# Moving transfers, waits and pieces of work at the layer ends of a two-layer attention and delta-rule trunk

## The reference

```python
mod = silu(c) @ w_ada + b_ada                 # shift, scale, gate; a second set from c_ctx
p   = (rmsnorm(x) * (1 + sc) + sh) @ w_in     # one projection for both groups of heads
# group A, 8 heads: differential softmax attention with rotary positions, SiLU gate
# group B, 8 heads: short convolution, chunked gated delta rule in both directions, SiLU gate
x   = x + gt * (concat([y_a, y_b]) @ w_out)   # the same for ctx, in the first layer only
```

## Time and profile before

| | |
|---|---|
| median of three runs | 2666.12 us (2658.32 to 2667.49) |
| the profiled execution, its own time | 2668.75 us |
| its span in the profile | 2666.9 us |
| granted TensorE clock, mean | 0.952 |
| busy share of PE, DVE, ACT, POOL | 89%, 53%, 35%, 4% |
| HBM traffic over the span | 123 GB/s |

### The profile page before, as it was taken

One profiled execution on the slowest core, in us unless ns is written; L12 is line 12 of the kernel. 1 busy time (PEld: TensorE's weight loads), 2 busy tenths in 40 slices (PEclk: granted clock), 3 DMA queues, 4 the chain that ended last, 5 costly groups with the idle time before them and its releaser, 6 DMA issues. The chain is left out here.

```text
span 2666.9 us, 40817 instructions
## 1 busy us (share of the span) xinstructions
PE 2373.2 (89%) x14870; PEld 1958.8 (73%) x14870; DVE 1413.2 (53%) x2409; ACT 924.6 (35%) x1727; POOL 102.3 (4%) x155
## 2 busy tenths in 40 slices
PE   6799999999989998999899689889898989889696
PEld 3278787878777877778688468778687877778685
DVE  1334646454555546464653554655666555655555
ACT  3434233242424242332412354242423424242422
POOL 0000000000000000000000000000000000000000
PEclk8999999999999999999899799999999999999897
DMA  8964444443434344443434445243433334233353
GB/s 322 353 174 120 112 121 107 112 123 99 119 91 127 84 116 106 127 107 95 150 112 146 150 107 141 68 115 79 111 99 92 97 88 125 74 102 84 114 154 123
DMA packets 553603, 329.72 MB, mean 124 GB/s; under 512 B 48658, under 2 KB 517814, under 8 KB 552710
## 3 DMA queue, kind: packets, MB, share of 16 engines
q1 hardware_dynamic: 393174, 218.59, 29.9%
q10 hardware_dynamic: 160240, 109.13, 14.1%
q0 software_dynamic: 64, 0.20, 0.0%
HBM read 304.73 MB, written 23.13 MB: 123 GB/s over the span
## 5 line engine op out<-in xcount | busy, mean ns | idle before, releaser
L1678 PE MATMUL ps<-h_hi,w_hi 128*128 128x512 f32 (+1 forms) x2080 | 835.2, 402 | 25.3 <-DVE h_lo L1037 12.6
L1679 PE MATMUL ps<-h_lo,w_hi 128*128 128x512 f32 (+1 forms) x2080 | 772.6, 371 | 0.0
L1680 PE MATMUL ps<-h_hi,w_lo 128*128 128x512 f32 (+1 forms) x2080 | 771.6, 371 | 0.0
L1037 DVE TENSOR_TENSOR w_lo<-w_raw,w_hi 128x1024 fp32r<-128x1024 f32 (+1 forms) x332 | 399.0, 1203 | 391.9 <-ACT w_hi L594 337.0
L594 ACT CAST w_hi<-w_raw 128x1024 fp32r<-128x1024 f32 (+1 forms) x332 | 341.2, 1030 | 544.5 <-PE ps L1680 153.7
L1678 PEld LDWEIGHTS ps<-h_hi,w_hi 128*128 128x128 f32 x2080 | 403.7, 194 | 121.1 <-issue 41.5
L1680 PEld LDWEIGHTS ps<-h_hi,w_lo 128*128 128x128 f32 x2080 | 401.8, 193 | 69.6
L1679 PEld LDWEIGHTS ps<-h_lo,w_hi 128*128 128x128 f32 x2080 | 404.8, 195 | 48.2
L1037 DVE TENSOR_TENSOR arena<-arena,ps 128x512 f32<-128x512 f32 (+1 forms) x192 | 117.7, 641 | 131.9 <-PE ps L1763 130.7
L1931 PE MATMUL ps<-h_hi,w_hi 128*128 128x512 f32 (+1 forms) x448 | 159.1, 355 | 6.8 <-DVE arena L1493 6.8
L1762 PE MATMUL ps<-arena 128*128 128x128 f32 x512 | 111.5, 303 | 50.7 <-DVE arena L1037 26.2
(11 more groups left out here) (189 smaller groups left out, 2738.9 us busy)
## 6 DMA issues: line engine op xcount, KB each, us to landing
w_raw<-in_w_in SPq DMA_DIRECT2D x260, 512.0 KB, 4.2
ada_raw<-in_w_ada ACTq DMA_DIRECT2D x128, 512.0 KB, 5.3
w_raw<-in_w_out SPq DMA_DIRECT2D x64, 448.0 KB, 3.8
arena<-in_w_ada SPq DMA_DIRECT2D x27, 512.0 KB, 8.3
w_raw<-in_w_ada SPq DMA_DIRECT2D x19, 512.0 KB, 8.3
ada_raw<-in_w_ada SPq DMA_DIRECT2D x18, 512.0 KB, 8.3
arena<-decay_rows ACTq DMA_DIRECT2D x16, 512.0 KB, 4.8
x_channel_major<-arena ACTq DMA_DIRECT2D x1, 4096.0 KB, 17.6
```

The lines of the kernel that those rows point to most:

```text
L1037: return V.tensor_tensor(o, a, b, op)
L1678: mm(o, w_hi[:, s, k], h_hi[:, kt, t0:], start=kt == 0, stop=False)
L1679: mm(o, w_hi[:, s, k], h_lo[:, kt, t0:], start=False, stop=False)
L1680: last = mm(o, w_lo[:, s, k], h_hi[:, kt, t0:], start=False, stop=kt == KT - 1)
```

## The change

- Order on SP: the block writes go from before unit 6 to before unit 7, `blocks_back` from before unit 8 or 9 to before unit 10; in the last body from after units 5 and 9 to after 7 and 11 (layer 0) or 8 and 13 (layer 1).
- `ADA_SLOT` of layer 0: 19, 44, 50 and 56 become 18, 46, 51 and 57.
- Last body: the pieces are spread from slot 2 on, not 8, and stand behind the plan of a slot on PE; the first four units are taken as half 0 of tiles 0 and 1, then half 1 of both. Groups 0 and 1 of y are loaded one unit earlier than groups 2 and 3, which need the last unit used; the splits of y move from slots 3, 4, 6, 7 to 0, 1 (2 on DVE), 4, 6.
- x blocks use four buffers in `ada_raw` in place of two in the arena. Blocks 0 to 7 of x are loaded for the tail in slot 38 of the last body (`old_load`).
- POOL sums the squares in place of DVE.
- Layer 1: the split of unit `base + 3` moves ahead of the modulation, and PE multiplies the first tile of body 0 (AV, units `base + 2` and `base + 3`) block by block beside the decay tile; slots 0 to 7 of body 0 project nothing.

Only added and removed lines are shown, with the line number of the kernel before.

```diff
@@ 238 @@
-x_part = (cin.rearrange("p s n -> p (s n)")[:, 0:T], th)
+x_part = [ada_raw[:, s // 2, 4 * (s % 2):4 * (s % 2) + 4].rearrange("p k n -> p (k n)") for s in range(4)]
@@ 426 @@
-ADA_SLOT, ADA_EARLY = {0: (9, 14, 19, 44, 50, 56), 1: (10, 17)}, {0: 3, 1: 2}
-BLOCKS_OUT, BLOCKS_BACK = {0: 6, 1: 6}, {0: 8, 1: 9}
+ADA_SLOT, ADA_EARLY = {0: (9, 14, 18, 46, 51, 57), 1: (10, 17)}, {0: 3, 1: 2}
+BLOCKS_OUT, BLOCKS_BACK = {0: 7, 1: 7}, {0: 10, 1: 10}
...
+def out_unit(u):
+    return (u % 2, u // 2) if u < 4 else (u // 2, u % 2)
+def last_unit(n):
+    return n + 2 if n < 2 else 2 * n + 1
...
-    return 8 + p * (SLOTS - 8) // (2 * OUT_UNITS)
+    return 2 + p * (SLOTS - 2) // (2 * OUT_UNITS)
...
-    return min(piece_slot(4 * n + 3) + 1, SLOTS - 1)
+    return min(piece_slot(2 * last_unit(n) + 1) + 1, SLOTS - 1)
+OUT_BLOCKS = {0: (7, 11), 1: (8, 13)}
@@ 549 @@
-half, n = u % 2, u // 2
+n, half = out_unit(u)
...
-    sp.wait_ge(w_used, first)
-    sp.wait_ge(ya_stored, 16 * (HEADS * layer + OUT_HEADS))
-    sp.wait_ge(yb_stored, 16 * (HEADS * layer + OUT_HEADS))
...
+        if g == 0:
+            sp.wait_ge(w_used, first - 1)
+            sp.wait_ge(ya_stored, 16 * (HEADS * layer + OUT_HEADS))
+        if g == 2:
+            sp.wait_ge(w_used, first)
+            sp.wait_ge(yb_stored, 16 * (HEADS * layer + OUT_HEADS))
...
-if u == 5:
+if u == OUT_BLOCKS[layer][0]:
...
-if u == 9:
+if u == OUT_BLOCKS[layer][1]:
@@ 665 @@
+    split_hi(0, base + LEAD)
...
-    for u in range(1, LEAD):
+    for u in range(1, LEAD + 1):
...
-split_hi(0, base + LEAD)
@@ 907 @@
+    act.wait_ge((ya_ready, yb_ready)[which], h())
...
-        act.wait_ge(qkv_ready, h(-1, 3, 3))
-        act.wait_ge(z_ready, h(-1, 2, 2))
...
-    if n >= 2:
-        act.wait_ge(part_stored[n % 2], 16 * (layer * KT // 2 + n // 2))
-    act.dma_start(x_part[n % 2][:, c0 * P:], x_dram[n, :, c0 * P:]).then_inc(part_loaded[n % 2], 16)
+    if n >= 4:
+        act.wait_ge(part_stored[n % 4], 16 * (layer * KT // 4 + n // 4))
+    act.dma_start(x_part[n % 4][:, c0 * P:], x_dram[n, :, c0 * P:]).then_inc(part_loaded[n % 4], 16)
+def old_load():
+    act.wait_ge(z_ready, h(-1, 2, 2))
+    for b in range(4):
+        act.wait_ge(part_stored[b], 16 * (layer * KT // 4 + 2))
+    for g in range(2):
+        load_old(g)
...
-    act.dma_start(x_dram[n, :, c0 * P:], x_part[n % 2][:, c0 * P:]).then_inc(part_stored[n % 2], 16)
+    act.dma_start(x_dram[n, :, c0 * P:], x_part[n % 4][:, c0 * P:]).then_inc(part_stored[n % 4], 16)
@@ 930 @@
-put(2, part_load, 0)
-put(2, part_load, 1)
+for n in range(4):
+    put(0, part_load, n)
...
-    put((3, 4, 6, 7)[g], y_hi, g)
-put(40, y_hi_last, 0)
+    put((0, 1, 4, 6)[g], y_hi, g)
+put(TURN_OA[layer] + 2, y_hi_last, 0)
+put(38, old_load)
@@ 975 @@
-if n + 2 < KT:
-    put(min(out_slot(n) + 2, SLOTS - 1), part_load, n + 2)
+if n + 4 < KT:
+    put(min(out_slot(n) + 2, SLOTS - 1), part_load, n + 4)
@@ 988 @@
+def load_old(g):
+    ks = slice(4 * g, 4 * g + 4)
+    act.dma_start(xT[:, ks, c0 * P:], x_dram[ks, :, c0 * P:].rearrange("k p t -> p k t")).then_inc(old_loaded[g], 16)
@@ 996 @@
-for b in range(2):
-    act.wait_ge(part_stored[b], 16 * (layer + 1) * KT // 2)
+for b in range(4):
+    act.wait_ge(part_stored[b], 16 * (layer + 1) * KT // 4)
...
-for g in range(4):
-    ks = slice(4 * g, 4 * g + 4)
-    act.dma_start(xT[:, ks, c0 * P:], x_dram[ks, :, c0 * P:].rearrange("k p t -> p k t")).then_inc(old_loaded[g], 16)
+for g in range(2, 4):
+    load_old(g)
@@ 1137 @@
+split_lo(0, base + LEAD)
...
-for u in range(1, LEAD):
+for u in range(1, LEAD + 1):
@@ 1414 @@
-vec.wait_ge(part_loaded[n % 2], 16 * (layer * KT // 2 + n // 2 + 1))
-vec.wait_ge(w_used, first + 2 * n + 2)
-add_product(n, x_part[n % 2])
+vec.wait_ge(part_loaded[n % 4], 16 * (layer * KT // 4 + n // 4 + 1))
+vec.wait_ge(w_used, first + last_unit(n) + 1)
+add_product(n, x_part[n % 4])
@@ 1426 @@
-    put((3, 4, 6, 7)[g], y_lo, g)
-put(40, y_lo_last, 0)
+    put((0, 2, 4, 6)[g], y_lo, g)
+put(TURN_OA[layer] + 2, y_lo_last, 0)
@@ 1498 @@
-split_lo(0, base + LEAD)
...
-def add_square(n):
-    vec.wait_ge(x_squared, layer * KT + n + 1)
-    tt(sq_sum[:, c0 * P:], sq_sum[:, c0 * P:], sq_tiles[n % 2][:, c0 * P:], ALU.add).then_inc(sums_ready, 1)
-    vec.wait_ge(sums_ready, layer * KT + n + 1)
@@ 1520 @@
-    if n >= 1:
-        add_square(n - 1)
-add_square(KT - 1)
@@ 1581 @@
+for n in range(KT):
+    pool.wait_ge(x_squared, layer * KT + n + 1)
+    G.tensor_tensor(sq_sum[:, c0 * P:], sq_sum[:, c0 * P:], sq_tiles[n % 2][:, c0 * P:],
+                    ALU.add).then_inc(sums_ready, 1)
+    pool.wait_ge(sums_ready, layer * KT + n + 1)
@@ 1669 @@
-def unit_piece(u, bank_, t0, half, ks, signal=None):
+def unit_piece(u, bank_, t0, half, ks, both=False):
...
-        mm(o, w_hi[:, s, k], h_lo[:, kt, t0:], start=False, stop=False)
+        before_last = mm(o, w_hi[:, s, k], h_lo[:, kt, t0:], start=False, stop=False)
...
-    return last
+    return (before_last, last) if both else last
...
-    pe.wait_ge(w_split, base + half + 1)
+    pe.wait_ge(w_split, base + half + (3 if layer else 1))
...
+        if k == HALF - 1:
+            last.then_inc(w_used, 1)
+        if layer:
+            before_last, last = unit_piece(base + 2 + half, PJ + 1, tokens(layer, 0), half, [k], both=True)
+if layer:
+    before_last.then_inc(w_used, 1)
@@ 1916 @@
-u, half, n = first + p // 2, p // 2 % 2, p // 4
+u = first + p // 2
+n, half = out_unit(p // 2)
...
-if p % 4 == 0 and n >= 2:
+if p % 2 == 0 and half == 0 and n >= 2:
@@ 1935 @@
-if not project:
-    for p in range(2 * OUT_UNITS):
-        if piece_slot(p) == s:
-            out_piece(p)
-if project:
+if project and not (layer and isinstance(i, int) and i == 0 and s < 2 * SLOTS // UNITS):
@@ 1952 @@
+if not project:
+    for p in range(2 * OUT_UNITS):
+        if piece_slot(p) == s:
+            out_piece(p)
```

More of the change, by code:

```diff
@@ L374, in build_trunk @@
         last_product = sem("last_product")
-        part_loaded = [sem(f"part_loaded{b}") for b in range(2)]
-        part_stored = [sem(f"part_stored{b}") for b in range(2)]
+        part_loaded = [sem(f"part_loaded{b}") for b in range(4)]
+        part_stored = [sem(f"part_stored{b}") for b in range(4)]
         old_loaded = [sem(f"old_loaded{g}") for g in range(4)]
```

## The result

The changed kernel takes 2585.06 us (median of four runs, 2583.03 to 2587.97); the kernel before took 2666.8 us beside it. The ratio is 0.9685, with an interval of 0.9648 to 0.9722: faster by 3.15%. 2558 was predicted, 2520 to 2625 the range; the time that rival A gave, 2603, lies nearer to the measured one than the forecast does. The profiled execution took 2584.58 us with a span of 2582.8, 84.1 us less than the span of before.

A forecast was written before the change was run, and what follows sets the result against it. PE was taken as the bound, so only its idle time and half clock could be gained. Terms 56 + 17 + 9 + 6 + 5 + 12 + 3 = 108 us off 2668.75 gave 2560.8, as median 2558 us; range 2520 to 2625.

The forecast's parts named there:

- rival A: Layers 0 and 1: the moved waits only move PE's stall to L1753, the turned inverse; 2603 us, chance 27%.
- Part 1: Layer 1's seven filled bodies: block steps moved behind weight loads save 8 us a body, 56 us; bounds 0 and 76.
- PE waits about 1 us for the turned inverse and as much for the mask: Layer 1's bodies: waits left to PE, taking the ceiling of 10.8 us down to 8 us a body.
- Part 2: Layer 0's seven filled bodies: block steps and adaLN slots moved save 2.5 us a body, 17 us; bounds -15 and 35.
- between -2 and +2 us a body; I take 0: Layer 0's bodies: net of PE waiting for the inverse, turned at 880 to 884, instead of for `mod`.
- Part 3: End of layer 0: output pieces start earlier, after early y loads, saving 9 us; bounds 5 and 13.
- PE still waits about 3 us: End of layer 0: wait left before the first output piece, while ACT handles x before emptying ZB.
- Part 4: Tail of layer 0: squares off DVE and x blocks loaded early save 6 us; bounds 0 and 16.
- Part 5: Layer 1's modulation: AV tile multiplied there, 48 matmuls leave body 0, saving 5 us; bounds 0 and 11.
- Part 6: End of layer 1: earlier output pieces and later block steps save 12 us, bounds 4 and 20; its tail 3 us.
- Rival C: Both layers: the solved blocks' store starts behind loads, its 8.3 us round trip doubles; slower, about 2707 us, chance 5%.
- the signs listed: Layer 1's L1627, L1762 under 1.5 us a body; layer 0's L1618 gone; output pieces within 4 us of v's last transposes.

The follow-up runs named there:

- The run with 9: Changed kernel with layer 0's `blocks_back` before unit 9 in place of unit 10: 2548.52 us, ratio 0.9527 to the kernel before.
- the last run: Layer 1's last-body block steps after units 7 and 11, not 8 and 13, against the kernel storing x two slots later (2520.58 us): 2534.72 us.

## Why the prediction was right, and which terms were mis-sized

The sign and the range held, and in layer 1's bodies the mechanism: PE is the bound, and what it gained are stalls whose cause was a load behind a wait on SP. Elsewhere the steps failed in part. The sum was 108, the profile shows 84: part 1 brought 12 us more than its term and the others together 36 less, so the total is as near as it is by luck in part. By term:

- **Part 1**, 56, measured 68.2. The step "PE waits about 1 us for the turned inverse and as much for the mask" was too careful: 0.2 us (1.4 / 7) and 0.9 us (6.1 / 7). It came to 9.7 us a body of the ceiling of 10.8, 6.1 of it idle time and 3.7 shorter busy time; the ceiling had 7.4 and 3.4. ACT's wait for `w_raw` in the stretch is 29.3 us in place of 59.9.
- **Part 2**, 17, measured 3.1: the largest miss. The step that failed is "between -2 and +2 us a body; I take 0". Its pieces were about right: the store "at about 872" on the old axis came at 872.8 (875.52 less the 2.76 us by which this body begins later), though the split came 0.6 us earlier and not "perhaps 1.4", and the round trip of 8.3 us with "its company up to 4 more" was 11.5. But put together they give 884.3 for the turned inverse, the late end of "880 to 884", and I had set that end equal to only 2 us of loss. PE's wait went from 3.5 to 7.4 us a body. The run with 9 shows the whole of it as 36.5 us. The other step was too careful: the move from 44 to 46, 51 and 57, taken at 16, is worth about 25 with unit 9, and the 0.2 us for "the next load, which has one slot less" show nowhere; no product behind slot 46 waits for its load. The load of slot 18, which this part counted among the company of the blocks, costs some 16 us with unit 9.
- **Part 3**, 9, measured 4.7. "PE still waits about 3 us" is 5.50 us; another 2.3 us of waits came inside, up to the tail (180 us stretch: 177.93 busy). The "some 2 us of half clock and shorter waits" were 2.7: 2.1 us of small waits beside the one of 9.83, and 0.6 us of busy time. ACT's copy and the low part of y are ready within 2 us of each other, so neither alone gives it back.
- **Part 4**, 6, measured 2.3. The 3.9 us for squares were worth nothing: DVE was not what paced the tail. The 2 us for early x loads were 3. POOL's addition, taken at 1.0 us, takes 1.28 against DVE's 0.69, a ratio of 1.9; the rule of the Trainium skill (GPSIMD Engine Reference, 4.1 Engine selection: about twice as slow for two inputs) is borne out by the trace. At the end, where only the last addition shows, the last product to the rms matmul takes 2.4 us in layer 1 with POOL in every run and 2.3 with DVE; in layer 0 the two can't be told apart (3.5 to 3.9 and 3.2 to 3.6 us). So the 0.3 us a layer were not seen.
- **Part 5**, 5, measured 4.2, right for a wrong reason. The uncovered decay chain costs 7.05 us, as put ("about 7"), but the tile itself brings no more than 0.5 us, less than the runs differ by; the split, which I had said "hides", is what is left to explain the rest.
- **Part 6**, 12 and 3, measured 1.5 and 2.2. The waits named are gone or smaller (L1931 for x, L1845 for ACT), and the last run shows that 8 and 13 are worth over 12 us against 7 and 11. But I took freed waits for gained time: in the same body came 7.5 us at L1865, 4.1 at L1959 for y and 3.8 at L1797. Of these the run with the x stores later takes off only half of the last; the other two stay. The one at L1865 grows to 16.7 us when the block steps come earlier; beyond that their cause is open. In layer 1 PE idled 31.8 us from the last turning to the tail before, 31.0 after, and 26.6 with the stores later.

Rival A (the stall only moves to L1753) came true in layer 0 and not at all in layer 1; I had given it one chance for both. Rival C's mechanism, the store behind the loads, was real in layer 0, at 4.6 us and not 8.3. A row of the kernel before had the price of a place behind SP's own load, 3.60 us for the round in layer 0's last body; the prediction did not use it. Of the signs listed, ACT's wait, L1627, L1762, L1618 and POOL's time came as put; output products within 4 us of the transposes did not (5.5 and 5.1).

## What to carry to other kernels

Moving a wait on a queue is two edits: what stood behind it is freed, and it now stands behind something itself. Place it by time, not by unit: if the awaited data is there before the load ahead of it can be issued, it comes too late (layer 0, unit 10), if it comes long after, all loads behind it starve (layer 1's end, unit 11); here unit 10 gained 68 us in one layer and cost 36 in the other against unit 9. For a short round trip look at other queues as well, and when an in-order engine is idle at an instruction that does not need what it waited for, look one instruction back.

## What the runs showed of the hardware that was not expected

- A small store (64 KB) and its completion take 1.92 to 1.96 us in nearly every body when nothing is ahead, in both layers; 5.9 to 6.8 us behind a 512 KB load issued 0.4 us earlier, with a 1 MB load of another queue beside it; 3.60 us behind a 448 KB load issued 0.4 us earlier without the 1 MB; 1.95 again when the 512 KB load had 3.5 us of lead.
- Behind such a load the store landed 0.2 us after it in six of eight bodies (0.9 and 1.3 us in the others). The 512 KB load takes 4.0 us with nothing beside it and 5.9 to 6.9 us beside the 1 MB.
- The 1 MB load on another queue alone stretches the store to between 2.17 and 5.31 us (mean 3.77); issued 0.5 us before the load it took up to 4.10 us, issued after it 3.39 at least.
- Eight small reads are turned 5.0 us after the first is issued in layer 1 and in the changed kernel's layer 0, and 7.1 to 9.1 us after it when a 1 MB load on another queue is issued between 0.25 us ahead of the first and 1.5 us behind it.
